# Second layer: attention heads and gated mixers without the queries of the 16 prefix tokens

## The reference, cut to what matters

```python
h = concat([meta, x])                     # 272 tokens
for layer in range(2):
    u = rmsnorm(h)
    ... = split(u @ w_in[layer])
    o_mla  = mla_branch(...)              # 8 heads, softmax(q k^T / sqrt(96)) v, causal
    o_gla  = gla_branch(...)              # 4 heads, chunked gated linear attention
    o_hgrn = hgrn2_branch(...)            # 4 heads, the same recurrence, other gates
    mixed = sum over branches of sigmoid(gate) * (o_branch @ w_branch)
    h = h + mixed @ w_out[layer]
    h = h + (swiglu(...) if layer == 0 else moe_swiglu(...))   # top-2 of 8 experts
return h[:, N_META:]
```

## Time and profile before

| | |
|---|---|
| median of 3 runs | 1855.7 us (1854.08 to 1856.85) |
| the profiled execution's own time | 1856.12 us |
| its span, first to last instruction | 1854.4 us |
| TensorE, VectorE, ScalarE busy | 97%, 81%, 69% of the span |
| first layer, to the second norm | 0 to 555 us |
| second layer's mixers and dense jobs | 555 to 860 us |
| last products, router, gathering | 860 to 898 us |
| expert loop | 898 to about 1845 us |

### The profile page before, as it was taken

How to read it: one execution, slowest core, us unless ns; L and a number is a source line. 1 busy time by engine, 2 the same in 40 slices (tenths; PEclk the granted TensorE clock), 3 DMA queues, 4 the chain that set the end, 5 groups by cost and what they waited for, 6 DMA issues and landing times.

```text
span 1854.4 us, 29579 instructions
## 1 busy us (share of the span) xinstructions
PE 1803.0 (97%) x10738; PEld 1573.2 (85%) x10738; DVE 1493.6 (81%) x1785; ACT 1285.0 (69%) x1637; POOL 88.7 (5%) x78
## 2 busy tenths in 40 slices
PE   8999999999989999999999999999999999999998
PEld 7888888999989887889888888888888888888886
DVE  7868787777548688777788988888888888898897
ACT  6767766544346776875677877778777777777776
POOL 0000001100010000002100100001000010000101
PEclk9999999999999999999999999999999999999999
DMA  6323324555453333336799999999999999999995
GB/s 223 125 92 126 114 92 148 171 172 177 161 197 124 105 119 109 125 104 235 309 373 371 403 370 375 392 371 396 370 369 400 368 393 377 361 406 366 367 403 213
DMA packets 87109, 485.38 MB, mean 262 GB/s; under 512 B 11646, under 2 KB 11950, under 8 KB 43744
## 3 DMA queue, kind: packets, MB, share of 16 engines
q1 hardware_dynamic: 83936, 476.01, 68.0%
q0 software_dynamic: 2944, 8.09, 1.7%
q10 hardware_dynamic: 144, 0.13, 0.0%
HBM read 477.17 MB, written 8.41 MB: 262 GB/s over the span
## 4 chain that ended last, share of the span: by engine, by line
PE 79%; DVE 12%; ACT 6%; issue 3%; DMA 0%; SPq 0%; POOLq 0%; DVEq 0%; ACTq 0%
PE bank L1810 11%; PE bank L1809 11%; PE bank L1814 11%; PE bank L1506 8%; PE bank L1508 7%; PE bank L1507 7%; PE bank L1827 5%; PE bank L1826 5%; PE bank L1832 5%; DVE lo L985 2%; ACT hi L671 2%; PE bank L1841 1%; PE bank L1683 1%; DVE qk L1177 1%; DVE qsq L1010 1%
## 5 line engine op out<-in xcount | busy, mean ns | idle before, releaser
L1335 DVE TENSOR_TENSOR mlo<-mraw,mhi 128x2048 fp32r<-128x2048 f32 x282 | 641.4, 2290 | 95.8 <-ACT mhi L870 83.0
L870 ACT ACTIVATE mhi<-mraw 128x2048 fp32r<-128x2048 f32 x283 | 540.6, 1916 | 107.7 <-PE bank L1832 50.5
L1506 PE MATMUL bank<-UH,hi 128*128 128x272 f32 (+1 forms) x1024 | 311.2, 304 | 15.8 <-DVE UL L998 5.4
L671 ACT ACTIVATE hi<-raw 128x1024 fp32r<-128x1024 f32 (+1 forms) x220 | 229.2, 1043 | 107.7 <-PE bank L1508 106.3
L1809 PE MATMUL bank<-mhi,xh 128*128 128x512 f32 x768 | 303.5, 395 | 0.0
L1810 PE MATMUL bank<-mhi,xl 128*128 128x512 f32 x768 | 299.5, 390 | 0.0
L985 DVE TENSOR_TENSOR lo<-raw,hi 128x1024 fp32r<-128x1024 f32 (+1 forms) x220 | 265.4, 1211 | 42.1 <-ACT hi L671 41.6
L1508 PE MATMUL bank<-UH,lo 128*128 128x272 f32 (+1 forms) x1024 | 294.8, 288 | 0.0
L1507 PE MATMUL bank<-UL,hi 128*128 128x272 f32 (+1 forms) x1024 | 293.9, 287 | 0.0
L1814 PE MATMUL bank<-mlo,xh 128*128 128x512 f32 x896 | 239.9, 389 | 0.0
L1506 PEld LDWEIGHTS bank<-UH,hi 128*128 128x128 f32 x1024 | 194.0, 189 | 28.3 <-issue 23.4
(11 more groups left out here) (347 smaller groups left out, 2934.4 us busy)
## 6 DMA issues: line engine op xcount, KB each, us to landing
mraw<-in_w_exp SPq DMA_DIRECT2D x336, 1024.0 KB, 5.6
raw<-in_w_dense SPq DMA_DIRECT2D x212, 512.0 KB, 3.3
raw<-in_w_dense SPq DMA_DIRECT2D x8, 384.0 KB, 3.1
wuq<-in_w_uq SPq DMA_DIRECT2D x2, 1024.0 KB, 8.6
hT<-in_tokens SPq DMA_DIRECT2D x4, 272.0 KB, 3.8
wukv<-in_w_ukv SPq DMA_DIRECT2D x2, 512.0 KB, 9.0
u_rows<-utok SPq DMA_DIRECT2D x1, 1024.0 KB, 4.9
y_rows<-acc SPq DMA_DIRECT2D x1, 1024.0 KB, 4.3
```

Source lines behind the costliest of these rows:

```text
L671: A_(hi[g % HI][:, 0:n], raw[g % RAW][:, 0:n], ACT.Copy).then_inc(hi_made, 1)
L870: A_(mhi[k % MHI][:], mraw[k % MRAW][:], ACT.Copy).then_inc(mhi_made, 1)
L1335: TT(mlo[k % MRAW][:], mraw[k % MRAW][:], mhi[k % MHI][:].bitcast(F32), ALU.subtract).then_inc(mlo_made, 1)
L1506: MM(ps, h, xh_, start=first, stop=False)
```

## The change

In the second layer (`asks(1)` is 16, `asks(0)` is 0) these are left out for each head: L1594, L1185, L1190, L797, L1195, L803 and L1602 in attention, and L1675, L1280, L1681, the third of each of L860 and L1285, and L1693 in the mixers. The copies and products over 272 columns that only carry queries (L1198, L1201, L1295, L811, L1204 and the prefix part of L1610) are cut to 256. Semaphore increments move to the instruction that is now last of its step. Keys, values and states are built over all 272 tokens as before. Order of jobs and steps, buffers and transfers are the same.

```diff
+def asks(layer):
+    return META if layer == DEPTH - 1 else 0
...
                     st(A_(pr[:, p, 0:272], pr[:, p, 0:272], ACT.Exp, bias=mx[:, p, 0:1], accum_out=sm[:, p, 0:1]))
...
-                    A_(pr[0:META, p, 416:432], pr[0:META, p, 416:432], ACT.Exp, bias=mx[0:META, p, 2:3],
-                       accum_out=sm[0:META, p, 2:3]).then_inc(mla_act, 1)
...
+                    if asks(layer) == 0:
+                        st(ins)
+                        ins = A_(pr[0:META, p, 416:432], pr[0:META, p, 416:432], ACT.Exp, bias=mx[0:META, p, 2:3],
+                                 accum_out=sm[0:META, p, 2:3])
+                    ins.then_inc(mla_act, 1)
...
-                    for n, rows in enumerate((P, P, META)):
+                    for n, rows in enumerate((P, P) if asks(layer) else (P, P, META)):
                         st(A_(ob[0:rows, i % 2, n * P:(n + 1) * P], L[0:rows, n * P:(n + 1) * P], ACT.Square,
...
-                    st(STT(pr[0:META, p, 416:432], Ma[0:META, 416:432], QK ** -0.5, mask[0:META, 416:432],
-                           ALU.mult, ALU.add))
+                    if asks(layer) == 0:
+                        st(STT(pr[0:META, p, 416:432], Ma[0:META, 416:432], QK ** -0.5, mask[0:META, 416:432],
+                               ALU.mult, ALU.add))
...
-                    CP(OT[:, i // 2, :], bank[2][:, 0:T]).then_inc(mla_dve, 1)
+                    CP(OT[:, i // 2, asks(layer):], bank[2][:, asks(layer):T]).then_inc(mla_dve, 1)
...
-                    MM(Ma[:, 272:416], q_[:, 16:144], k_[:, 0:144], start=True, stop=True)
-                    MM(Ma[0:META, 416:432], q_[:, 0:16], k_[:, 0:16], start=True, stop=True).then_inc(mla_psum, 1)
+                    ins = MM(Ma[:, 272:416], q_[:, 16:144], k_[:, 0:144], start=True, stop=True)
+                    if asks(layer) == 0:
+                        ins = MM(Ma[0:META, 416:432], q_[:, 0:16], k_[:, 0:16], start=True, stop=True)
+                    ins.then_inc(mla_psum, 1)
...
-                    MM(L[0:META, 256:384], AT[0:META, i % 2, 256:272], V0[:, h], start=True, stop=True)
+                    if asks(layer) == 0:
+                        MM(L[0:META, 256:384], AT[0:META, i % 2, 256:272], V0[:, h], start=True, stop=True)
...
-                        TR(L[:, c0:c0 + P], ob[:, i % 2, n * P:(n + 1) * P], ident)
-                    TR(L[:, 0:META], ob[0:META, i % 2, 256:384], ident[0:META, 0:META]).then_inc(la_psum, 1)
+                        ins = TR(L[:, c0:c0 + P], ob[:, i % 2, n * P:(n + 1) * P], ident)
+                    if asks(layer) == 0:
+                        ins = TR(L[:, 0:META], ob[0:META, i % 2, 256:384], ident[0:META, 0:META])
+                    ins.then_inc(la_psum, 1)
```

More of the change, by code:

```diff
@@ L810, in mla @@
                     act.wait_ge(stream_done, J(layer, "wo", 11)["part"] + 2)
-                    A_(OH[:, i, :], OT[:, i, :], ACT.Copy).then_inc(mla_act, 1)
+                    A_(OH[:, i, asks(layer):], OT[:, i, asks(layer):], ACT.Copy).then_inc(mla_act, 1)
             def la(unit, name, i):
@@ L1202, in mla @@
                 elif name == "ot":
                     dve.wait_ge(mla_act, N(layer, name, i, "act"))
-                    TT(OL[:, i, :], OT[:, i, :], OH[:, i, :].bitcast(F32), ALU.subtract).then_inc(mla_dve, 1)
+                    c = slice(asks(layer), T)
+                    TT(OL[:, i, c], OT[:, i, c], OH[:, i, c].bitcast(F32), ALU.subtract).then_inc(mla_dve, 1)
             def la(unit, name, i):
@@ L1278, in la @@
                     for n in range(2):
-                        st(E.copy_predicated(AT[:, i % 2, n * P:(n + 1) * P], m, L[:, n * P:(n + 1) * P]))
-                    E.copy_predicated(AT[0:META, i % 2, 256:272], m[0:META, 0:META],
-                                      L[0:META, 256:272]).then_inc(la_dve, 1)
+                        ins = E.copy_predicated(AT[:, i % 2, n * P:(n + 1) * P], m, L[:, n * P:(n + 1) * P])
+                        if n == 0:
+                            st(ins)
+                    if asks(layer) == 0:
+                        st(ins)
+                        ins = E.copy_predicated(AT[0:META, i % 2, 256:272], m[0:META, 0:META], L[0:META, 256:272])
+                    ins.then_inc(la_dve, 1)
                 elif name == "o":
                     dve.wait_ge(la_act, N(unit, name, i, "act"))
-                    for n, rows in enumerate((P, P, META)):
+                    last = 1 if asks(layer) else 2
+                    for n, rows in enumerate((P, P, META)[:last + 1]):
                         ins = TS(ob[0:rows, i % 2, n * P:(n + 1) * P], L[0:rows, n * P:(n + 1) * P],
                                  rl[0:rows, i % 2, n:n + 1], None, ALU.mult)
-                        if n < 2:
+                        if n < last:
                             st(ins)
@@ L1294, in la @@
                     where = O[:, 0, i, :] if u == 0 else O[:, 1, 2 * (u - 1) + i, :]
-                    TS(where, L[:, 0:T], g, None, ALU.mult).then_inc(la_dve, 1)
+                    TS(where[:, asks(layer):], L[:, asks(layer):T], g, None, ALU.mult).then_inc(la_dve, 1)
             E.memset(ez[:], 0.0).then_inc(zero_made, 1)
@@ L1600, in mla @@
                     TR(Ma[0:META, 144:272], pr[:, p, 0:16], ident)
-                    TR(Ma[0:META, 16:144], pr[:, p, 272:288], ident)
-                    TR(Ma[0:META, 0:16], pr[0:META, p, 416:432], ident[0:META, 0:META]).then_inc(mla_psum, 1)
+                    ins = TR(Ma[0:META, 16:144], pr[:, p, 272:288], ident)
+                    if asks(layer) == 0:
+                        ins = TR(Ma[0:META, 0:16], pr[0:META, p, 416:432], ident[0:META, 0:META])
+                    ins.then_inc(mla_psum, 1)
                 elif name == "pv":
@@ L1605, in mla @@
                     pe.wait_ge(mla_dve, N(layer, "pt", i, "dve"))
-                    for b, (lo_, n, keys) in enumerate(((0, META, ptm), (META, P, ptf), (META + P, P, ptf))):
+                    for b, (lo_, n, keys) in enumerate(((asks(layer), META, ptm), (META, P, ptf), (META + P, P, ptf))):
                         for q in range(2):
                             c = slice((i - 1 + q) * VDIM, (i + q) * VDIM)
-                            w_ = (slice(0, T), slice(0, 256), slice(256, 384))[b]
+                            w_ = (slice(asks(layer), T), slice(0, 256), slice(256, 384))[b]
                             ins = MM(bank[2][VDIM * q:VDIM * q + VDIM, lo_:T], vtok[0:n, b, c], keys[0:n, q, w_],
@@ L1673, in la @@
                         c = slice(CH + n * P, CH + (n + 1) * P)
-                        MM(L[:, n * P:(n + 1) * P], KE[a:b, t, c], QE[a:b, t, c], start=True, stop=True)
-                    MM(L[0:META, 256:272], KE[a:b, t, OFF:CH], QE[a:b, t, OFF:CH],
-                       start=True, stop=True).then_inc(la_psum, 1)
+                        ins = MM(L[:, n * P:(n + 1) * P], KE[a:b, t, c], QE[a:b, t, c], start=True, stop=True)
+                    if asks(layer) == 0:
+                        ins = MM(L[0:META, 256:272], KE[a:b, t, OFF:CH], QE[a:b, t, OFF:CH], start=True, stop=True)
+                    ins.then_inc(la_psum, 1)
                 elif name == "o":
```

29 lines of the change are left out of this document (19 added, 10 removed).

## The result

The changed kernel takes 1845.8 us in the median of 6 runs (1844.8 to 1847.0), the one before 1855.8 us (6 runs, 1854.1 to 1858.4). The ratio is 0.9947, 95% interval 0.9937 to 0.9957. The forecast was 1845.7 us. Its profiled execution has a span of 1844.7 us, against 1854.4.

A forecast was written before the change was run, and what follows sets the result against it. Engines bound 555 to 860 us in turns (TensorE, ScalarE, VectorE). The terms 0.7 + 3.2 + 1.1 + 1.7 + 0.7 + 1.7 + 0.5 + 0.3 + 0.1 = 10.0 us took 1855.7 to 1845.7 us, range 1842.0 to 1850.5.

The forecast's parts named there:

- The turns: Between 555 and 860 us engines set the end in turn; a saving counts only on the engine whose turn it is.
- ScalarE's 0.7 us before 619: 555 to 619.03 us: ScalarE's two exponentials and smaller passes removed before the copy of `V` save 0.7 us.
- TensorE's 3.2 and ScalarE's 1.1 us up to 704.8: Removed small products and transposes save 3.2 us from 619 to 664.7; removed exponentials and scalings 1.1 us to 704.8.
- The first `o` behind its wait, 0.3 us: Near 738 and 804 us: the first L1681, behind the wait for mask L1280, is worth only 0.3 us each time.
- 1.4 + 0.7 and 1.4 + 0.5 us: 738.3 to 770.1 and 804.0 to 827.0 us: TensorE's savings without the first `o`, then ScalarE's.
- The end, 0.3 us: 827.0 to 860 us, TensorE's turn: one L1602 (0.28 us) and a `pv` save 0.3 us.
- Own slots only: Rival: removed TensorE instructions save only their own start-to-start slots, late starts stay; 7.8 us saved, 1847.9 us; chance 0.20.
- the long form: A removed small TensorE shape also saves the next instruction's late start: 0.40 us for L1681, 0.36 for L1693.
- The slower rival: Rival: idler TensorE brings clock falls inside the mixers, 3.4 us each; four would give 1859.3 us; chance 0.04.

The follow-up runs named there:

- e1: Changed kernel with ScalarE's and VectorE's part undone, so only TensorE leaves out the second layer's prefix queries; 1848.3 us.
- e2: Changed kernel with TensorE's part undone, so only ScalarE and VectorE leave out the second layer's prefix queries; 1852.2 us.
- e5: Changed kernel with the 16-row transpose L1693 put back in the second layer's eight mixer heads, its result unread; 1847.6 us.
- e6: Changed kernel with an unread full 128 x 128 transpose where the 16-row L1693 had been; 1845.2 us.
- e3: Changed kernel with the mixers' part undone, so only the second layer's attention heads leave out prefix queries; 1852.9 us.
- e4: Changed kernel with attention's part undone, so only the second layer's gated mixers leave out prefix queries; 1848.1 us.
- e10: The changed kernel itself, unaltered, measured and profiled once more for its clock; 1844.7 us.
- e7: Changed kernel with the prefix queries left out in the first layer too, which makes the output another one; 1834.2 us.
- e8: Changed kernel with all of `rc`'s scalings of the probabilities moved from ScalarE to GpSimd in both layers; 1837.4 us.
- e9: Kernel of e8 with the product of keys and decays (128 x 640) also moved from VectorE to GpSimd, both layers; 1834.3 us.

## Why the prediction was right

- *What bounds the kernel.* The turns were read rightly. e1 and e2 moved the waits that the prediction gave to each engine, and from 619 us on their sum is the whole within 0.02 us in each stretch without a fall (e1's and the changed kernel's at 676 us set aside).
- *ScalarE's 0.7 us before 619.* Right: 0.71 in both profiles, counted from where the clock is back. The raw 1.02 of the first profile would have flattered it. The sign named for it, a wait for `V` 0.7 us shorter, came as 0.59.
- *TensorE's 3.2 and ScalarE's 1.1 us up to 704.8.* 4.3 together, 4.47 measured; apart, 3.43 in e1 and 1.03 in e2. What was too low is TensorE's term, and in it L1681. The prediction read its late start up to the next product's first record, 0.40 us; up to the product behind, it is 0.51. Starts of the two traces set side by side give 0.51 + 0.33 + 0.49 + 0.50 = 1.8 us for the four L1681 of this turn, where 1.5 were put, while the four L1675 kept their own slots (0.12 to 0.16 us) and L1693 gave 0.33, the last one partly hidden as forecast (e5 gives back 0.87 us for the three). The prediction said that VectorE's chain of norms keeps its length and the gaps widen; they did (1.12 to 1.83 at `O`), as did the wait for `AT` (0.31 to 1.06) to which L1675 of units 4 and 5 went.
- *The first `o` behind its wait, 0.3 us.* 0.40, 0.03 of it `pv`'s: the product of `o` starts 0.05 us behind the end of the last 128-row mask (733.81 and 733.86) where it started 0.43 us behind it (738.17 and 738.61). The mask's 16 x 16 part and the small product are both gone from the way.
- *1.4 + 0.7 and 1.4 + 0.5 us.* 2.19 and 1.96: 0.1 us off each. In e2 ScalarE's shares are 0.68 and 0.48, as forecast; TensorE's are 1.52 and 1.49 in e1 where 1.4 were put, which is again the 0.1 us by which L1681 was read too short.
- *The end, 0.3 us.* 0.51, so mis-sized by 0.2. By the starts, L1602 with `pv` gave the 0.3 us as forecast; 0.12 more is the wait for `rt` in the router (0.48 to 0.36 us), of which the prediction says nothing, and the rest are steps of 0.03 us. Why that wait is shorter wasn't tried.
- *Own slots or the long form.* The long form, for L1693 by e5 and e6 and for L1681 by the 0.12 us in the trace, and longer yet. "Own slots only" would have left 1847.9 us, outside the interval of the ratio (1844.1 to 1847.8 us) by little; the starts decide it, not the time.
- *The clock.* Half right. "TensorE ran at full clock in all these stretches" was true of the one execution that was read and is no property of the kernel. The slower rival's mechanism did appear: the wait for `O` grew, and the clock fell behind it. It cost nothing, because the fall lies in VectorE's turn. Three things were read or argued wrongly on the way. The prediction said against that rival that the gaps stay no longer than they are, though its own sum has two of them widen. Its row for TensorE's idleness "before" the fall at the norm, 547.00 to 554.30 us, holds 4.63 us of the fall itself; in the 2.67 us before it TensorE was busy for 0.72. And it priced the fall of 6.8 us at the gathering at 3.4 us; executions without one (e3, e4, e6, e10) are 2.2 to 2.5 us shorter from there to the end.

The last point can be read off two rows, of the changed kernel and of e7, which has the same wait of 1.83 us at that place and no fall behind it. The changed kernel's row at 676.40 stands above; e7's for the same work, 0.4 us behind the end of its wait, is

```profile
664.40:667.80 3.40, 2.67 (x24) 2.50 (x22) 3.30 (x9) 1.48 (x5) 0.00 (x0) 1.00 0.00 0
```

In both VectorE is busy for 3.30 of 3.40 us. At 0.51 of the clock TensorE is busy for all of it, at full clock for 2.67, and then it waits (0.72 and 0.50 us at the next two waits for `O`, which are absent in the changed kernel). The fall filled idle time. The stretch from 619 to 704.8 says the same: e7 has no fall there and wins 4.43 us, e3 and e4 have none and win 4.44 together, and the changed kernel has one and wins 4.47.

The sum of the terms was 10.0 us; the stretches add up to 0.71 + 4.47 + 0.40 + 2.19 + 0.40 + 1.96 + 0.51 = 10.6 us. The medians lie 10.0 us apart. That the time was hit to 0.1 us is partly luck: the terms are 0.6 us too low together, and falls of the clock move a single execution by more than that. The span, too, came within 0.3 us (1844.7, forecast 1844.4) only because 1.14 us lost in the first layer stand against 10.95 us won between the norm and the gathering.

## What to carry to other kernels

Cut a stage into turns by the waits that end last, and credit a saving only on the engine whose turn it is; if the cuts are right, the parts undone one by one add up to the whole, which is a cheap test. Read what a matmul costs from start to start including its successor's late start, above all where a few-row shape stands between full ones. Read on to the second instruction behind it: 0.1 us of L1681's cost lay there. Where ScalarE or VectorE has the turn and GpSimd is idle, moving a pass there can pay though GpSimd needs two to four times as long: e8 won 3.4 of the 4.1 us of scalings that it took off ScalarE in the second layer. And where the clock changes between executions, cut behind its falls before you compare a stretch.

## What the runs showed of the hardware that was not expected

- A 16-row transpose between 128-row instructions costs TensorE 0.35 us, a full 128-row one at the same place 0.11 us (e5, e6). A 16 x 16 x 128 product behind a dense matmul costs 0.51 us up to the second product behind it, and 0.33 us behind another narrower product (before against the changed kernel).
- The granted clock falls to 0.50 for 3.4 us, or two or three times that, also inside busy stretches and not in every execution. At 676 us a fall follows the wait of 1.83 us for `O` in the changed kernel (both profiles), e1, e6, e8 and e9, and not in e7 with the same wait; no profile with a wait of 1.12 to 1.66 us there (before, e2 to e5) has it. Others stood at 253 us (changed kernel, e3, e4), at 772 to 790 us behind TensorE's wait of 1.58 to 1.61 us for `KLT` (e1, e2, e3, e7, e10; the same wait in before, e4, e5, e6, e8 and the first profile of the changed kernel has none behind it), and around the gathering for 6.8, for 3.4 or for no us.
- What a fall costs depends on whose turn it is: nothing that shows at 676; 0.8 us at 783 in e10; up to 2.5 us at the gathering, by which the stretch from there to the end is shorter in e4, which has no fall there. Why some executions have one and others none was not settled.
- GpSimd's scaling of 128 x 272 took 0.97 us in five of its executions in e8's second layer and 1.68 to 2.00 in three, beside a busy VectorE.
